# Tokens passed in two groups: row gathers beside the second group's trunk, dense experts on 320 of 640 tokens

## The reference, cut to what matters

```
p  = x @ w_in                                  # q, k, v of two mixers, and two gates
yA = chunk-band attention (16 heads of 64);  yB = sliding-window attention, 2 key heads, sinks
h  = LN1(alpha*x + (sigmoid(gA)*(yA@w_proj_a) + sigmoid(gB)*(yB@w_proj_b)) @ w_out)
# PEER: 8 heads, each picks 16 of 128*128 experts through two tables of 128 keys
s1, s2 = q @ keys1, q @ keys2 ; top 16 of each ; top 16 of the 256 sums ; gate = softmax
act = gelu(u_table[experts] . h)               # 128 rows of 2048 a token
y  = LN2(alpha*h + sum(gate * act * v_table[experts]))
```

## Time and profile before

| | us |
|---|---|
| median of 3 runs (lowest, highest) | 4462.09 (4461.21, 4473.39) |
| span of the profiled execution, first to last instruction | 4456.8 |
| trunk, to the end of the queries | 14 to 2107 |
| 20 early u units, then gate matrix with the last of them | 2107 to 2191, 2191 to 2391 |
| rest of the experts, gathers beside them | 2391 to 4386 |
| last LayerNorm and stores | 4386 to 4456 |

### The profile page before, as it was taken

One profiled execution on the slowest core, in us unless ns is written; L12 is line 12 of the kernel. 1 busy time (PEld: TensorE's weight loads), 2 busy tenths in 40 slices (PEclk: granted clock), 3 DMA queues, 4 the chain that ended last, 5 costly groups with the idle time before them and its releaser, 6 DMA issues.

```text
span 4456.8 us, 71381 instructions
## 1 busy us (share of the span) xinstructions
PE 4282.4 (96%) x26508; PEld 4120.7 (92%) x26508; DVE 2839.1 (64%) x4233; ACT 1376.0 (31%) x2750; POOL 2672.1 (60%) x1665
## 2 busy tenths in 40 slices
PE   8999999999989999799899999999999999999998
PEld 8999888878879999699899999999999999999997
DVE  1000133444442231699997899898997988988988
ACT  1000122222221110311386434343443443443444
POOL 5444322222324545244776778778887888888884
PEclk9999999999999999999999999999999999999999
DMA  5222233222233323112489999999999999999995
GB/s 202 99 102 98 96 119 128 104 81 81 78 119 122 116 90 99 38 66 76 145 276 320 382 376 398 374 372 409 416 405 377 412 418 411 417 411 416 418 418 241
DMA packets 269138, 1083.82 MB, mean 243 GB/s; under 512 B 24560, under 2 KB 90224, under 8 KB 185328
## 3 DMA queue, kind: packets, MB, share of 16 engines
q0 software_dynamic: 74736, 544.24, 29.8%
q1 hardware_dynamic: 89568, 391.16, 23.6%
q10 hardware_dynamic: 104736, 147.39, 9.7%
HBM read 1020.44 MB, written 67.63 MB: 244 GB/s over the span
## 4 chain that ended last, share of the span: by engine, by line
PE 66%; DVE 18%; DMA 6%; issue 5%; POOL 3%; ACT 1%; ACTq 0%; DVEq 0%; POOLq 0%
PE banks L497 30%; PE banks L741 15%; PE banks L675 11%; DVE work L1499 3%; DVE work L1462 2%; DVE banks L1465 2%; POOL w_lo L383 2%; PE banks L729 2%; DMA work<-in_u_rows,idx_all 2%; PE banks L566 2%; PE banks L528 2%; DMA work<-in_v_rows,idx_all 1%; POOL work L411 1%; PE banks L536 1%; DVE work L1371 1%
## 5 line engine op out<-in xcount | busy, mean ns | idle before, releaser
L383 POOL TENSOR_TENSOR w_lo<-w_raw,w_hi 128x1024 fp32r<-128x1024 f32 x472 | 1140.7, 2417 | 243.5 <-ACT w_hi L1057 229.6
L389 POOL TENSOR_SCALAR w_hi<-w_raw 128x2048 fp32r<-128x2048 f32 x134 | 289.6, 2161 | 1326.8 <-PE banks L497 1252.3
L497 PE MATMUL banks<-mv_hi,w_hi 128*128 128x256 f32 x3648 | 863.2, 318 | 62.9 <-DVE mv_lo L1203 35.4
L497 PE MATMUL banks<-mv_lo,w_hi 128*128 128x256 f32 x3648 | 835.8, 310 | 0.0
L497 PE MATMUL banks<-mv_hi,w_lo 128*128 128x256 f32 x3648 | 835.3, 310 | 0.0
L497 PEld LDWEIGHTS banks<-mv_hi,w_hi 128*128 128x128 f32 x3648 | 652.1, 189 | 127.1 <-issue 85.9
L741 PE MATMUL banks<-mv_hi,w_hi 128*128 128x384 f32 x2048 | 693.2, 338 | 43.5 <-ACT part_t L1116 22.1
L393 POOL TENSOR_TENSOR w_lo<-w_raw,w_hi 128x512 fp32r<-128x512 f32 x536 | 721.0, 1377 | 11.2
L675 PE MATMUL banks<-mv_hi,w_hi 128*128 128x384 f32 x2048 | 694.0, 339 | 4.6 <-ACTq L1083 2.0
L741 PE MATMUL banks<-mv_lo,w_hi 128*128 128x384 f32 x2048 | 690.3, 337 | 0.0
L741 PE MATMUL banks<-mv_hi,w_lo 128*128 128x384 f32 x2048 | 690.3, 337 | 0.0
(11 more groups left out here) (166 smaller groups left out, 5319.5 us busy)
## 6 DMA issues: line engine op xcount, KB each, us to landing
w_raw<-in_wstream SPq DMA_DIRECT2D x472, 512.0 KB, 7.9
w_raw<-in_wstream SPq DMA_DIRECT2D x134, 1024.0 KB, 4.8
gate_matrix<-work ACTq DMA_DIRECT2D x12, 2048.0 KB, 9.0
work<-gate_matrix ACTq DMA_DIRECT2D x32, 768.0 KB, 9.0
out_p<-work ACTq DMA_DIRECT2D x34, 320.0 KB, 2.2
work<-out_p ACTq DMA_DIRECT2D x34, 320.0 KB, 3.4
gate_scratch<-work ACTq DMA_DIRECT2D x32, 320.0 KB, 2.2
work<-gate_scratch ACTq DMA_DIRECT2D x16, 640.0 KB, 4.0
```

The lines of the kernel that those rows point to most:

```text
L383: pool.tensor_tensor(w_lo[s][:, part], raw[s][:, part], w_hi[s][:, part].bitcast(f32), ALU.subtract) \
L389: pool.tensor_scalar(w_hi[s][:, :], raw[s][:, :], 1.0, 0.0, ALU.mult, ALU.add).then_inc(hi_done, 1)
L497: last = pe.matmul(acc(dst, h), a[s][:, P * k:P * k + P], b[h][:, k, :], start=(k == k_first and n == 0), stop=(k == k_last and n == 2))
```

## The change

1. **Two groups.** Tokens 0 to 255 pass the trunk alone (`WIDTH[0]` = 256), then tokens 256 to 639 (`WIDTH[1]` = 384). All 114 trunk units are loaded and split twice. Ten of the second group's q, k, v units stand as filler between the stages of the first group, 24 behind its queries.
2. **Gathering starts early.** The list of gather steps now begins in the 13th of those 24 units and runs beside the second group's attention (3 a unit), projections, output and early u units.
3. **64 more tokens are gathered** in a third, packed block (each half of the partitions takes half of a token's 128 picks), so 640 gathers instead of 512; dense experts run on 320 tokens (`ND`).
4. **Expert stage.** Groups of eight rows of 128 experts (`EG` = 8): a v unit gives two sums instead of four, and VectorE adds them straight from PSUM. 48 u units run early instead of 20, the last 20 of them beside the gate matrix (80 steps instead of 96). The gate matrix's groups of the early units come last.
5. **Split.** ScalarE now makes every `w_hi`, in halves, and GpSimd only `w_lo`. Attention is software-pipelined over pairs, with loads of the next pair ahead, three softmax buffers, and for the second group one score bank.

The core of the diff:

```diff
-N1 = 2 * P
-N2 = T - N1
-WAVES = ((0, N1), (N1, N2))
+WIDTH = (2 * P, T - 2 * P)
+FROM = (0, 2 * P)
...
-EG = 4
+G3 = 64
+ND = WIDTH[1] - G3
+EG = 8
...
+SEGMENTS = (("qkv", U_QKV, N_QKV), ("gate", U_GATE, N_GATE),
+            ("b0", U_QKV, 2), ("proj", U_PROJ, N_PROJ),
+            ("b1", U_QKV + 2, 2), ("out", U_OUT, N_OUT),
+            ("b2", U_QKV + 4, 2), ("b3", U_QKV + 6, 4), ("query", U_QUERY, N_QUERY),
+            ("b4", U_QKV + 10, 24), ("gate_b", U_GATE, N_GATE), ("proj_b", U_PROJ, N_PROJ),
+            ("out_b", U_OUT, N_OUT), ("query_b", U_QUERY, N_QUERY), ("peer", U_PEER, 2 * KEYS))
...
+GATHER_AT = AT["b4"] + 12
+RATES = ((GATHER_AT, AT_GATE[1], 2.4), (AT_GATE[1] + 1, AT_PROJ[1], 3.0), (AT_PROJ[1], AT_OUT[1], 2.0),
+         (AT_OUT[1], AT_QUERY[1], 1.6), (AT_EARLY + GEXP_AT, AT_EARLY + TAIL, 1.9), (AT_EARLY + TAIL, AT_LATE, 1.0))
...
-                for n, (a, b) in enumerate(((w_hi, mv_hi), (w_hi, mv_lo), (w_lo, mv_hi))):
-                    for h in range(2):
-                        last = pe.matmul(acc(dst, h), a[s][:, P * k:P * k + P], b[h][:, k, :],
-                                         start=(k == k_first and n == 0), stop=(k == k_last and n == 2))
+                for n, (a, b) in enumerate(((w_hi, mv_hi), (w_hi, mv_lo), (w_lo, mv_hi))):
+                    ins = pe.matmul(out, a[s][:, P * k:P * k + P], b[ph][:, k, :],
+                                    start=(k == first and n == 0), stop=(k == last and n == 2))
...
+            def add_out(q, n, dt):
+                dve.wait_ge((half_read, unit_done)[dt % 2], n + 1)
+                dve.tensor_tensor(r_acc[:, dt, :], bank_of(dt), r_acc[:, dt, :], ALU.add).then_inc(out_evac, 1)
```

More of the change, by code:

```diff
@@ L647, in _ @@
[L647 to L657 removed]
+                    pe.wait_ge(r_done, 2 * i + (18 * ph + s + 1))
```

2549 lines of the change are left out of this document (1383 added, 1166 removed).

## The result

| | before | after |
|---|---|---|
| median us (lowest, highest) | 4465.24 (4461.21, 4473.39) | 4522.47 (4520.74, 4525.46) |
| ratio after/before, 95% interval | | 1.0126 (1.0111, 1.0140) |
| span of the profiled execution | 4456.8 | 4519.0 |

The change makes the kernel 1.3% slower. The forecast was 4311, so the sum is short by 213 us of span (4519 against 4306).

A forecast was written before the change was run, and what follows sets the result against it. TensorE was taken to bound the kernel, hiding a full DMA system that would pace the last units. Terms 1151 + 952 + 443 + 1700 + 60 gave 4306, with 5.3 around it 4311 us; range 4170 to 4425.

The forecast's parts named there:

- DMA gives way: Rival, last 208 units: DMA carries more than the slices show, time 4170 or 4075 us; 10 in 100.
- the lower rate: Rival, last 208 units: the end's DMA mix holds only 380 GB/s, 1829 us, time 4440; 3 in 100.
- the end: Last 208 units: 695 MB at 411 GB/s is 1691 us, plus 9 for short packets: 1700.
- the first attention: Group one's gates and attention: gates 184 us plus 145 of attention's own time, 329.
- the second attention: Group two's gates and attention with gathers: 96 steps of 4.95 us plus 10, 485 (451 to 540).
- VectorE becomes the bound by a little: Second attention: VectorE needs 4.95 us a step against TensorE's 4.7.
- attention as a chain: Rival, second attention: row steps lie in the chain from scores to values, 7.1 us a step, 4505; 6 in 100.
- Start: Group one's q, k, v: start 14, 34 units 196, plus 7 us lost before, 217.
- Tail: After the last 208 units: 60 us, before 70.
- The rivals that ended above before: Slower than before: attention as a chain, 4505 us; 6 in 100.
- the joints cost: Rival: 256-token splits, second attention's upper bound and stage-change waits give 60 to 130 more, 4370 to 4440; 12 in 100.
- The whole trunk is a wash: Trunk of both groups ends at 2103 us, before 2107; attention's row steps give back what overlap saves.

The follow-up runs named there:

- x3_light: Changed kernel, second half of each weight unit of the last 208 loaded with only 64 of 1024 columns (result wrong): 4396.15 us.
- x4_few: Changed kernel, third block gathering 4 instead of 64 picks a table, 120 row steps fewer: 4315.75 us.
- b1_before_light: Kernel before, second half of each of its last 176 weight units loaded with only 64 of 1024 columns: 4458.32 us.
- x5_acts_early: Changed kernel, stored activations' loads issued one slot earlier, in the group before, and their products moved to slots 3 to 6: 4488.26 us.
- c6_spread_more: c5_spread with 8 row steps moved from the regular to the last 48 units: 4422.31 us, ratio 0.9887.
- x8_chunk: Changed kernel, first attention's gate k-steps dealt 10, 5, 6, 11 instead of 8 each around the small matmuls: 4507.85 us.
- x2_att_loads: Changed kernel, ScalarE's issues at each attention's start reordered: first loads and gate split ahead of the wait for the last stores: 4501.91 us.
- x6_no_gather_att: Changed kernel without row steps beside the second attention, its 93 gathers dealt to later units: 4723.86 us.
- x7_tbanks: Changed kernel, first attention's transposes alternating between two PSUM banks instead of one: 4476.84 us.
- c5_spread: x5_acts_early with its loads issued two a slot over slots 4 to 7, plus x7_tbanks and x2_att_loads: 4407.78 us, ratio 0.9864.
- x10_last_fewer: x5_acts_early with 0.6 gather steps a unit fewer in the last 48 units, dealt to the 160 regular ones: 4528.57 us.
- c3_comb3: Changed kernel with x7_tbanks, x5_acts_early and x2_att_loads together: 4427.05 us, ratio 0.9917.

## Why the prediction was wrong

**Right.** TensorE's pace: 710 matmuls of 256 columns in 85 us without a wait, 0.120, and 275 of 320 columns in 40 us, 0.1455:

```profile
660.00:745.00 85.00, 85.00 (x710) 85.00 (x709) 20.91 (x45) 41.09 (x45) 70.17 (x31) 1.00 0.75 223
...
2330.00:2370.00 40.00, 40.00 (x275) 40.00 (x274) 3.20 (x8) 16.71 (x20) 26.68 (x11) 1.00 0.61 174
```

The bytes of the last 208 units: 695 MB forecast, 543.25 + 151.32 = 694.6 in the trace. That DMA becomes the bound when matmuls get shorter: shown by x3_light and x4_few, and that TensorE hid it before by b1_before_light. VectorE does wait for rows there (187 + 146 us in the regular units). The rate without the last units: 405 GB/s where 411 was taken; this is +20 us of 1342, a small mis-sizing. "DMA gives way" fell. So did the lower rate as a property of the packets' mix. The Trainium skill's 358 GB/s (DMA: Bandwidth & Descriptors, Where 436 GB/s comes from) is not what this core shows, 405 over 1342 us. Its rule on two SBUF inputs (SBUF — State Buffer, Who interferes with whom) fits: in x5_acts_early's last units the addition of 128x320 from PSUM takes 0.48 us whether GpSimd splits weights beside it or not, while a product with both inputs in SBUF (L1799) takes 0.48 in the 29 cases without a split beside it and 1.80 in the mean of the 11 with one.

**Wrong, the end (+117).** The step that failed is "*695 MB ... at 411 GB/s ... I add 9 for the short packets of the last 48 units*". A stage was priced by bytes over a rate, which holds only while there is always a row to fetch. In the last 48 units there is not: the forecast named no load of stored activations as a wait, although 48 of them stand there. Shown: 35 us by loads issued one slot earlier and used one slot later, 19 more by spreading them over the four slots ahead, which takes away the rest of VectorE's wait for them. What is left (417 against 392, the forecast's share for 48 units at 8.17) was not taken apart; a row step costs 3 us there by c6_spread_more.

**Wrong, the first attention (+74).** The step is "*of attention's own 368 I keep 330 ... and give group one 145*". Its gate units need 184, so its own part was 219. Shown: 45 us hang on the single transpose bank, which all transposes of a pair go through. Before had a single bank too (`t_bank`, bank 6), but with 14.07 us of long matmuls a unit around it where 5.76 stand now, and TensorE hardly ever waited for its copy; its waits in the attention of before began with

```profile
PE banks L536 <- DVE work L1251: 9.6, 16, 0.9
```

and had 3.4 us for a copy by ScalarE. A term scaled from a stage with long matmuls was taken to be a property of the small ones; it was in part a property of the cover. That is read from the two traces; the test is of the bank alone. The remaining 29 were not settled; x8_chunk and x2_att_loads gave 7 to 9, at the edge of what single executions tell.

**Wrong, the second attention (+43), with a mechanism that fell.** "*VectorE becomes the bound by a little*": it was busy 409 of 528, and without a single row step the stage still took 501. A term mis-sized: attention's own part is 501 - 266 = 235, not 185, of which 23 were a stop at its start, which x6_no_gather_att has too (x2_att_loads got 7 back). The other 27 are not accounted for one by one. The rival of attention as a chain fell as well: row steps cost 0.29 us each, not 2.4.

**Start (+17).** Not tested, but the trace of after shows the same pattern as at the start of the second attention. ScalarE issues its first loads in one burst from 14 to 44 us; of these the last eleven (the attention's biases) take 25 us to issue. Its next weight split and then TensorE wait behind it:

```profile
44.03 1.06 ACT L928 ACTIVATE w_hi<-w_raw 128x1024 fp32r<-128x1024 f32 x1 [27.77 <-issue]
47.67 0.55 PE L531 MATMUL banks<-mv,w_hi 128*128 128x256 f32 x1 [17.77 <-POOL w_lo L466]
```

Before issues such a burst as well (eight of these loads take 16.2 us), and TensorE did not stop: a unit gave it 14.07 us of work where it now gives 5.76. The forecast had 7 us for all waits of this stage.

**Tail (-30).** Not tested.

**The sign.** The rivals that ended above before had 6 in 100, all in one mechanism. The nearest rival was "the joints cost", and it ended below before: what came was larger than its bounds of 60 to 130, and only partly in its places (it had the second attention and waits at stage changes, not the first attention and not the loads of the last units). The clock was in no term: 390 us more at the lower level than before. It can't be added up as a loss, since much of it lies in the DMA-bound units, where it costs nothing; where TensorE is the bound it makes each short stop dearer, as x7_tbanks shows (18 us of listed waits, 45 of time). "The whole trunk is a wash" fell with the attention stages: it ends at 2232, not 2103.

## What to carry to other kernels

Before work is made shorter on the bounding engine, list every short wait that its length hid, and price each on its own: single buffers between two engines, bursts of DMA issues on an engine that also feeds the bound, loads issued a slot or two before their use. A stage that is paced by DMA is only as fast as its worst consumer in fixed order, for what DMA misses while that one stands is not made up. And place movable work by a measured price for each place: here a gather cost 0.3 us beside attention, 2.5 in a regular unit and 4 beside the queries, where the DMA share was only 0.37 but the order of GpSimd was in the way. Last, when an edit hits its forecast, look whether the wait that its theory names is the one that fell: c5_spread did what was expected of it, by another wait.

## What the runs showed of the hardware

- A burst of loads on ScalarE's queue blocks the engine: two issues took 8.3 us where the eight before them took under 0.5 each (after, second attention), and in another place eight took 6.3 (x10_last_fewer).
- Loads of 160 KB, eight in a row, landed 24.5 us after issue (median, c3_comb3's last units); two at a time they landed after 10.0 (c5_spread). Stores of the same size in the early units took 5.7 (after).
- A VectorE operation of 128x320 with both inputs in SBUF took 0.48 us without a GpSimd split beside it and 1.80 in the mean with one; with one input in PSUM 0.48 in either case (x5_acts_early).
- Light packets are not free: in b1_before_light the weights' queue moved 47% fewer bytes in as many packets, and its share of the DMA engines fell by 35%.
- Two stops of about 4 us at a joint had 16 matmuls 0.265 us apart between and behind them, until 8 us after the first stop, instead of 0.147. 48 us less of such time went with 18 us less of waits in the first attention.
